# Expert rows taken by one-hot products inside the expert loop, and the attention bias on VectorE, in a hybrid block with 32 experts

## The chip, the cores and the metric

One core of a Trainium2 chip runs the whole block in one launch. The metric is the device time in microseconds, as the median of several runs. All tensors are fp32 in HBM. The core has TensorE (PE, with its weight loads as PEld), VectorE (DVE), ScalarE (ACT), GpSimd (POOL) and the queue of SyncE (SP), which issues nearly all loads.

## The reference

256 tokens of width 1024 pass one layer: a norm, three branches (a short convolution, attention with 8 heads of 64, a gated linear attention), a gated merge, an output projection, and a mixture of 32 experts of which each token takes two.

```python
h = rms_norm(x, norm_mix); parts = split(h @ w_in)              # w_in: 1024 x 4624
# attention, causal, T = 256, one block
s = q @ k.T * scale + table[:, t5_bucket(q_pos - k_pos)]        # -inf above the diagonal
y_attn = softmax(s) @ v
merged = sum(sigmoid(h @ w_merge_gate[n]) * (y_n @ w_branch[n]) for n in 3 branches)
x = x + merged @ w_out
h2 = rms_norm(x, norm_ffn)
group = argmax(h2 @ w_rg + b_rg)                                # 4 groups of 8 experts
top_p, top_i = top_k(softmax(le of that group), 2)
weights = p_group_top * top_p / sum(top_p)
for each expert e, with xs = the rows of h2 that chose e:
    ys = (silu(xs @ w_g[e]) * (xs @ w_u[e])) @ w_d[e]           # 1024 -> 512 -> 1024
x = x + sum over the two choices of weights * ys
```

## The kernel before

It is written engine by engine, with semaphores by hand, so the order on each engine is the order of the text. Line numbers are those of the profile.

**The dense part.** Twenty weight matrices of 2 MB (L424 to L428) pass through five slots of SBUF, `ring`. ScalarE rounds each quarter to fp32r (`high_pre`, L700) and VectorE takes the rest (`low_pre`, L1404), and TensorE makes three fp32r products in place of one in fp32 (L988 to L990 by feature, L966 to L968 by token). Ten half-matrix products, `dense[u]`, are interleaved with the eight heads (L1131 to L1138). After each stand the scores of head u (`scores`), the transposes of the probabilities of head u-1 (`turn_prob`) and the products with v of head u-2 (`prob_v`). A head's scores are a product of a reversing matrix `antid` with the bias rows (L1103) and one of q and k (L1104), summed in PSUM. q is kept zero outside its head's 64 rows, so that these products use all 128 rows. VectorE takes the row maximum from PSUM (`row_max`, L1546), ScalarE the exponential, VectorE scales by the row sum (`prob_scale`, L1552, L1555).

**Output projection and routing.** `out_proj` (L1169 to L1171) writes four banks. VectorE adds them to x, TensorE transposes the new x (`turn_x1`) and multiplies it with the router's weights (`route`, L1193), VectorE picks the experts (`pick`), and small products count the slot of every choice (L1219), which VectorE reads as `slotf` (L1720). Slots are sorted by expert. `seed` (L1186) puts x into the four banks in which the result is summed.

**The gather.** VectorE builds two one-hot matrices of 128 tokens by 512 slots, `perm` (L1724, L1725). Eight groups of four fp32r products (L1253 to L1265) make x of all 512 slots, which ScalarE and VectorE copy to `xs`. Then in the loop GpSimd copies the 64 columns of each expert out of `xs` into `xe` (L660).

**The expert loop.** One pass runs over 32 experts. Each has six units of weights of 1 MB: gate and up in two halves, down in two halves. They land in a ring of 20 units (`unit`), in the order of `order` (L451 to L456). SP issues a load when the unit 20 places before has been used (`unit_free`). The first 20 loads (`first_load`) wait for the regions of SBUF that the dense part still holds. On TensorE one turn of the loop is: first half of gate and up of expert e (L1293, L1295, which write the two halves of the columns and so run side by side), the transposes of expert e-1's product (`turn_h`, L1308), the sums of expert e-2 into the four banks (`combine`, L1346), second half of gate and up, and the down products of expert e-1 (L1332; L1328 for the last).

Of the kernel before, what the change touches and what calls it, by code (L numbers as in the profile page):

```python
# [56 lines left out]
GATHER = (0, 1, 2, 0, 1, 2, 1, 2)  # L57
# [4 lines left out]
SPAD = SLOTS + WIN  # L62
# [14 lines left out]
RING = 20  # L77
# [19 lines left out]
def hybrid_block(nc, x, rel_bias_table, norm_mix, w_in, conv_w, conv_b, q_norm, k_norm, w_gla_alpha,  # L97
# [17 lines left out]
    with ctx:  # L115
# [26 lines left out]
        antid = place("antid", [P, P], F32)  # L142
# [24 lines left out]
        stat = place("stat", [P, 64], F32)  # L167
        reset = place("reset", [P, T], F32)
# [3 lines left out]
        rsum = place("rsum", [P, NH, TT], F32)  # L172

# [12 lines left out]
        iota_g = place("iota_g", [P, NE], F32)  # L186
        jcol = place("jcol", [P, MAXWIN], F32)
        slotf = place("slotf", [P, TT, TOPK], F32)
        wts = place("wts", [P, TT, 2], F32)
        offf = place("offf", [1, MAXWIN * NE + 1], F32)  # L190
        off_tab = place("off_tab", [1, MAXWIN * NE + 1], I32)
# [10 lines left out]
        here_at = [region]  # L202
        sig0 = here("sig0", [P, KD, T], F32)
# [14 lines left out]
        small_at = region + 6 * 4 * UNIT + 4 * KD * SPAD  # L218
        out_hi = [w_hi, [place(f"out_hi{c}", [P, CW], F32R, at=small_at + 4 * CW * c) for c in range(CHUNKS)]]
# [9 lines left out]
        gv_at = here_at[0]  # L229
        gv = here("gv", [P, TT, C], F32)  # L230
# [20 lines left out]
        here_at = [region]  # L251
        spare_at = [region, region + 4 * UNIT]
        here_at[0] += 2 * 4 * UNIT
        xs_at = here_at[0]
        xs = here("xs", [P, KD, SPAD], F32)
        fin = place("fin", [P, TT, D], F32, at=xs_at)
        spare_at += [here_at[0] + 4 * UNIT * i for i in range(4)]
        here_at[0] += 4 * 4 * UNIT
        xe = []
        for b in range(2):  # L260
            perm_at = here_at[0]
            xe.append(here(f"xe{b}", [P, KD, WIN], F32))
        back_at = here_at[0]
        assert back_at == small_at + 4096
        g_act = here("g_act", [P, C], F32)
        y_hi = here("y_hi", [P, C], F32R)
        w_hit = here("w_hit", [P, TOPK, T], F32)
        back = [here(f"back{b}", [P, T], F32R) for b in range(2)]
        assert here_at[0] == back_at + 4 * TT * D
        xn_hi = place("xn_hi", [P, TT, D], F32R, at=back_at)  # L270
        junk = place("junk", [P, D], F32, at=spare_at[0] + 4 * D)
        xn_lo = place("xn_lo", [P, TT, D], F32R, at=spare_at[0])
        he = here("he", [P, KC, WIN], F32)
        slot_row = here("slot_row", [P, TOPK, T], F32)
        perm = [place(f"perm{b}", [P, SLOTS], F32R, at=at) for b, at in enumerate((here_at[0], perm_at))]
        w_row = here("w_row", [P, TOPK, T], F32)
# [4 lines left out]
        iota_s = place("iota_s", [P, SLOTS], F32, at=w_al_at)  # L281
        y_lo = place("y_lo", [P, C], F32R, at=w_al_at)

        unit_at = [ring_at[s] + 4 * UNIT * j for s in range(3) for j in range(2)] + [spare_at[1]] + spare_at[2:]
        unit_at += [ring_at[3], ring_at[3] + 4 * UNIT, w_hi_at, w_hi_at + 4 * UNIT]
        unit_at += [ring_at[4], ring_at[4] + 4 * UNIT, xn_at, x_at, spare_at[0]]
# [42 lines left out]
        xn_lo_ready = sem("xn_lo_ready")  # L329
# [3 lines left out]
        xs_act = sem("xs_act")  # L333
        xs_dve = sem("xs_dve")
# [54 lines left out]
        perm_ready = sem("perm_ready")  # L389
        route_ready = sem("route_ready")  # L390
        gather_mm = sem("gather_mm")
        iota_ready = sem("iota_ready")
# [6 lines left out]
        seeded = sem("seeded")  # L399
        slot_ready = sem("slot_ready")  # L400
# [13 lines left out]
        first_act = sem("first_act")  # L414
        first_dve = sem("first_dve")
# [36 lines left out]
        for e in range(1, NE):  # L452
            halves = [[(kind, e, c) for kind in ("g", "u")] for c in range(2)]
            downs = [("d", e - 1, c) for c in range(2)]
            order += halves[0] + (downs + halves[1] if e == NE - 1 else halves[1] + downs)
# [96 lines left out]
        def _(pool):  # L552
# [80 lines left out]
            for h in range(NH):  # L633
                if h >= 4:
                    pool.wait_ge(score_mm, h - 3)
# [1229 lines left out]
```

## Time and profile before

| | |
|---|---|
| median of 3 runs | 764.85 us (764.61 to 765.08) |
| profiled execution | 764.3 us, of which the span is 762.6 us |
| PE busy | 689.7 us, 90% of the span |
| DVE, ACT, POOL busy | 303.3, 199.7, 44.4 us |
| moved by DMA | 247.39 MB |
| first gate product of expert 0 | 312.93 us from the start |

The profile shows one execution. "Busy" is the time in which an engine had an instruction in flight, and matmul ends are modelled, so that the distance between the starts of two matmuls says more than the duration of one. Each fp32 matmul leaves two records. 128\*64 behind a matmul means that it uses 128 rows and 64 columns of the array, 64\*128 means 64 rows and all columns. The chain is followed back from the last instruction, and names at each step what released it.

### The profile page before, as it was taken

What the parts mean: (1) busy time and instruction counts of PE and PEld (TensorE: products, weight loads), DVE (VectorE), ACT (ScalarE), POOL (GpSimd) and SP (SyncE); (2) the same over time, 40 slices, a digit from 0 to 9 for tenths busy, and PEclk for the clock granted to TensorE, in tenths of its full rate; (3) what the DMA queues carried; (4) which work ended last, traced back from release to release, by engine and by line L of the source; (5) the groups of instructions that cost most, each with busy time, mean ns of one, the idle gap of its engine ahead of it and who ended that gap; (6) DMA issues with size and microseconds to landing.
All of it is one profiled execution on the core that took longest, in us unless ns stands there. A gap on an engine that the chain in (4) does not pass through costs nothing.

```text
span 762.6 us, 10123 instructions
## 1 busy us (share of the span) xinstructions
PE 689.7 (90%) x3888; PEld 410.0 (54%) x3888; DVE 303.3 (40%) x512; ACT 199.7 (26%) x308; POOL 44.4 (6%) x89
## 2 busy tenths in 40 slices
PE   4999999999999999999999998798879888987895
PEld 3977799899999877533333333233323323332332
DVE  5357777754545666422322222311221212122212
ACT  4275355363434533211111111111011111111011
POOL 7002100000000000000000000000000000000000
PEclk9999999999999999999999999999999999999998
DMA  8963463454555389699999999999999999999993
GB/s 245 371 228 124 158 195 125 127 169 149 152 186 217 138 362 390 236 423 421 421 420 421 422 419 423 420 422 422 419 419 423 420 422 422 421 422 421 421 419 141
DMA packets 50175, 247.39 MB, mean 324 GB/s; under 512 B 5592, under 2 KB 5680, under 8 KB 25680
## 3 DMA queue, kind: packets, MB, share of 16 engines
q1 hardware_dynamic: 48672, 245.45, 81.2%
q0 software_dynamic: 912, 1.25, 0.9%
q8 instruction: 31, 0.51, 0.3%
q10 hardware_dynamic: 544, 0.06, 0.1%
q14 instruction: 16, 0.13, 0.0%
HBM read 245.67 MB, written 1.06 MB: 324 GB/s over the span
## 4 chain that ended last, share of the span: by engine, by line
PE 59%; DMA 29%; DVE 5%; SPq 3%; ACT 2%; issue 1%; DVEq 0%; ACTq 0%
DMA unit<-in_w_expert_up 28%; PE ps L1293 16%; PE ps L1332 7%; PE ps L988 6%; PE ps L990 6%; PE ps L989 6%; SPq L499 3%; PE ps L1346 2%; PE ps L966 2%; PE ps L968 2%; PE ps L967 2%; DVE ring_lo L1404 1%; ACT w_hi L700 1%; PE ps L1169 1%; PE ps L1171 1%
## 5 line engine op out<-in xcount | busy, mean ns | idle before, releaser
L1293 PE MATMUL ps<-unit,xe 128*64 128x512 f32 x512 | 245.2, 625 | 44.7 <-DMA unit<-in_w_expert_up 44.7
L1295 PE MATMUL ps<-unit,xe 128*64 128x512 f32 x512 | 246.0, 626 | 0.0
L1293 PEld LDWEIGHTS ps<-unit,xe 128*64 128x64 f32 x512 | 68.8, 142 | 194.4 <-issue 194.2
L1791 DVE TENSOR_TENSOR g_act<-g_act,ps 64x512 f32<-64x512 f32 x32 | 34.6, 1081 | 243.2 <-ACT g_act L889 240.0
L1404 DVE TENSOR_TENSOR ring_lo<-ring,w_hi 128x1024 fp32r<-128x1024 f32 x76 | 91.4, 1223 | 53.9 <-ACT w_hi L700 52.6
L1332 PE MATMUL ps<-unit,he 128*64 128x512 f32 x496 | 111.9, 592 | 0.0
L988 PE MATMUL ps<-hT_hi,w_hi 128*128 128x256 f32 x320 | 92.0, 287 | 2.7 <-DVE ring_lo L1404 2.7
L700 ACT ACTIVATE w_hi<-ring 128x1024 fp32r<-128x1024 f32 x76 | 79.0, 1057 | 47.3 <-PE ps L990 34.9
L989 PE MATMUL ps<-hT_lo,w_hi 128*128 128x256 f32 x320 | 90.5, 283 | 0.0
L990 PE MATMUL ps<-hT_hi,ring_lo 128*128 128x256 f32 x320 | 90.4, 283 | 0.0
L1332 PEld LDWEIGHTS ps<-unit,he 128*64 128x64 f32 x496 | 37.0, 137 | 69.2 <-issue 64.6
L1295 PEld LDWEIGHTS ps<-unit,xe 128*64 128x64 f32 x512 | 68.8, 142 | 0.0
L988 PEld LDWEIGHTS ps<-hT_hi,w_hi 128*128 128x128 f32 x320 | 61.3, 192 | 5.3 <-issue 5.1
L990 PEld LDWEIGHTS ps<-hT_hi,ring_lo 128*128 128x128 f32 x320 | 61.2, 191 | 0.0
L989 PEld LDWEIGHTS ps<-hT_lo,w_hi 128*128 128x128 f32 x320 | 61.2, 191 | 0.0
L1816 DVE SCALAR_TENSOR_TENSOR y_lo<-ps,w_slot,y_hi 128x512 fp32r<-128x512 f32 (+1 forms) x32 | 23.8, 742 | 88.1 <-ACT y_hi L907 88.1
L898 ACT ACTIVATE he<-ps 128x256 f32<-128x256 f32 x32 | 12.3, 385 | 154.8 <-PE ps L1308 154.8
L889 ACT ACTIVATE g_act<-ps 64x512 f32<-64x512 f32 x32 | 18.9, 589 | 129.5 <-PE ps L1295 129.5
L907 ACT ACTIVATE y_hi<-ps,w_slot 128x512 fp32r<-128x512 f32 (+1 forms) x32 | 21.8, 681 | 96.9 <-PE ps L1332 93.0
L660 POOL COPY xe<-xs 128x512 f32 x31 | 19.1, 616 | 398.7 <-PE ps L1295 380.7
L1346 PE MATMUL ps<-y_hi,back 64*128 64x512 f32 x128 | 34.6, 437 | 1.7 <-DVE y_lo L1821 1.7
L966 PE MATMUL ps<-w_hi,hT_hi 128*128 128x512 f32 x80 | 32.3, 404 | 1.3 <-DVE ring_lo L1404 1.2
(295 smaller groups left out, 799.2 us busy)
## 6 DMA issues: line engine op xcount, KB each, us to landing
unit<-in_w_expert_gate SPq DMA_DIRECT2D x64, 1024.0 KB, 26.9
unit<-in_w_expert_up SPq DMA_DIRECT2D x64, 1024.0 KB, 26.6
unit<-in_w_expert_down SPq DMA_DIRECT2D x63, 1024.0 KB, 26.6
ring<-in_w_in SPq DMA_DIRECT2D x9, 2048.0 KB, 14.2
ring<-in_w_merge_gate SPq DMA_DIRECT2D x6, 2048.0 KB, 10.7
ring<-in_w_branch SPq DMA_DIRECT2D x3, 2048.0 KB, 8.8
ring<-in_w_out SPq DMA_DIRECT2D x2, 2048.0 KB, 8.5
x_tok<-in_x SPq DMA_DIRECT2D x2, 512.0 KB, 4.4
```

The lines of the kernel that those rows point to most:

```text
L700: s_.activation(w_hi[c][:, :], ring[g % PRE_RING][:, chunk(c)], ACT.Copy).then_inc(wpre_hi, 1)
L966: t_.matmul(bank(b), x_hi[:, k, rows], wh, start=(k == 0), stop=False)
L988: t_.matmul(o, wh, x_hi[:, k, :], start=(k == 0 and j == 0), stop=False, skip_group_check=True)
L989: t_.matmul(o, wh, x_lo[:, k, :], start=False, stop=False, skip_group_check=True)
L990: ins = t_.matmul(o, wl, x_hi[:, k, :], start=False, stop=(k == nk - 1), skip_group_check=True)
L1293: gate = t_.matmul(ps[0:WIN, b, :], xe[b][:, k, :], ug[:, C * j:C * (j + 1)], start=(k == 0), stop=(k == KD - 1))
L1295: up = t_.matmul(ps[WIN:P, b, :], xe[b][:, k, :], uu[:, C * j:C * (j + 1)], start=(k == 0), stop=(k == KD - 1))
L1332: ins = t_.matmul(ps[half * WIN:(half + 1) * WIN, 3, :], he[:, k, :], u[:, D * j + C * half:D * j + C * (half + 1)], start=(k == 0), stop= ...
L1346: ins = t_.matmul(bank(4 + 2 * tt + half), back[e % 2][rows, tt * P:(tt + 1) * P], part[rows, :], start=False, stop=True, skip_group_check ...
L1404: v.tensor_tensor(ring_lo[g % PRE_RING][:, chunk(c)], ring[g % PRE_RING][:, chunk(c)], out_hi[g == 19][c][:, :].bitcast(F32), ALU.subtract ...
L1791: v.tensor_tensor(g_act[0:WIN, :].rearrange("p (k f) -> p k f", k=KC), g_act[WIN:P, :].rearrange("p (f k) -> p k f", k=KC), ps[WIN:P, e % ...
L1816: v.scalar_tensor_tensor(out=y_lo[:, 0:cols], in0=bank(3)[:, 0:cols], scalar=w_slot[:, e % 2:e % 2 + 1], in1=y_hi[:, 0:cols].bitcast(F32), ...
```

## The change

In the dense part:

- A pair of heads is computed together. Scores use 64 rows for each of the two heads, with no product for the bias. `row_max` is one VectorE instruction that adds the bias, writes the sum to SBUF and takes the maximum, and one that negates it. `scores` and `prob_v` run on every other turn. The order of queries is reversed in q and back in the result.
- In the linear attention the loops over the two row halves become inner loops.

At the output projection:

- The last of the four banks is computed as two of 256 columns, each added, squared and transposed by itself.
- The low part of the normed x is no longer made. x is scaled into `xn2` in fp32, in an order of columns in which each half of an expert's rows is contiguous.

At the experts:

- `perm`, `xs`, the eight gather groups and GpSimd's copies go. For each expert VectorE builds a one-hot matrix of 256 tokens by 64 places (`choose`), TensorE makes the 64 rows by four fp32 products (`pick_rows`), ScalarE copies them to SBUF (`rows_copy`), TensorE transposes them (`turn_rows`), and VectorE scales them into `xe` (`rows_in`). In the loop this is done for expert e+1 while expert e runs.
- The ring has 21 units at other addresses, and the first loads wait for other points.
- The last expert's order on TensorE and its order of loads are changed.

```diff
+            def pick_rows(i, e):
+                pe.wait_ge(chosen_ready, i + (e + 1))
+                for tt in range(TT):
+                    for c in range(2):
+                        ins = t_.matmul(ps[c * WIN:(c + 1) * WIN, e % 2, :], pick_w[e % 2][:, tt, :], xn2[:, tt, C * c:C * (c + 1)],
+                                        start=(tt == 0), stop=(tt == TT - 1))
+                ins.then_inc(picked, 1)
+            def turn_rows(i, e):
+                pe.wait_ge(rows_out, i + (e + 1))
+                pe.sem_inc(turning, 1)
+                for j in range(4):
+                    ins = t_.transpose(bank(e % 2, 4)[:, j, :], xr[:, j * P:(j + 1) * P], ident[:, :])
+                ins.then_inc(rows_turned, 1)
...
             with pe.Fori(0, passes) as p:
-                gate_up(p, 0, (0, 1))
+                gate_up(p, 0, (0,))
+                pick_rows(NE * p, 1)
+                gate_up(p, 0, (1,))
+                turn_rows(NE * p, 1)
...
                 for e in range(1, NE - 1):
                     gate_up(p, e, (0,))
                     turn_h(p, e - 1)
+                    pick_rows(NE * p, e + 1)
                     if e >= 2:
                         combine(p, e - 2)
                     gate_up(p, e, (1,))
+                    turn_rows(NE * p, e + 1)
                     down(p, e - 1)
                 gate_up(p, NE - 1, (0,))
                 turn_h(p, NE - 2)
                 combine(p, NE - 3)
-                down(p, NE - 2)
                 gate_up(p, NE - 1, (1,))
+                down(p, NE - 2, (0,))
+                turn_h(p, NE - 1)
+                down(p, NE - 2, (1,))
+                down(p, NE - 1, (0,))
                 combine(p, NE - 2)
-                turn_h(p, NE - 1)
-                down(p, NE - 1)
+                down(p, NE - 1, (1,))
                 combine(p, NE - 1)
...
+            def choose(i, e):
+                dve.wait_ge(picked, i + (e + 1))
+                v.scalar_tensor_tensor(out=both, in0=places, scalar=tab[:, 0, e:e + 1], in1=flat_slots, op0=ALU.add,
+                                       op1=ALU.is_equal).then_inc(same_ready, 1)
+                dve.wait_ge(same_ready, i + (e + 1))
+                v.tensor_tensor(pick_w[e % 2][:, :, :], same[:, :, 0, :], same[:, :, 1, :], ALU.add).then_inc(chosen_ready, 1)
+            def rows_in(i, e):
+                dve.wait_ge(rows_turned, i + (e + 2))
+                v.tensor_tensor(xe[e % 2][:, :, :, :], ps[:, e % 2, :].rearrange("p (j c n) -> p j c n", j=4, c=2),
+                                g_ffn[:, :].rearrange("p (c j) -> p j c", c=2).unsqueeze(3).broadcast_to([P, 4, 2, WIN]),
+                                ALU.mult).then_inc(xe_ready, 1)
...
                 for tt in range(TT):
-                    t_.matmul(o, antid[:, :], bias_h[:, h % 4, P * (1 - tt):T], start=True, stop=False)
-                    ins = t_.matmul(o, qTz[:, h, tt * P:(tt + 1) * P], kT[:, h // 2, keys], start=False, stop=True)
+                    for h in heads:
+                        rows = slice(DH * (h % 2), DH * (h % 2) + DH)
+                        ins = t_.matmul(ps[:, 4 + h % 2, P * tt:P + 2 * P * tt], qTz[rows, h, tt * P:(tt + 1) * P],
+                                        kT[rows, pair, 0:P * (tt + 1)], start=True, stop=True)
...
-                    ins = v.tensor_reduce(nmx[:, h, tt:tt + 1], ps[:, 4 + h % 2, P * tt:P + 2 * P * tt], AX_X, ALU.max,
-                                          negate=True)
+                    ins = v.tensor_tensor_reduce(prob[:, h % 2, P * tt:P + 2 * P * tt], ps[:, 4 + h % 2, P * tt:P + 2 * P * tt],
+                                                 bias_h[:, h % 4, P * (1 - tt):T], 1.0, -3e38, ALU.add, ALU.max,
+                                                 rmx[:, h, tt:tt + 1])
...
-                if n < 6:
-                    sp.wait_ge(proj_done, first_bank[NPRE - PRE_RING + n // 2 + 1])
+                if n < 5:
+                    sp.wait_ge(branch_done, 8)
                 elif n < 11:
+                    sp.wait_ge(proj_done, first_bank[NPRE - PRE_RING + (n - 5) // 2 + 1])
+                elif n == 11:
                     sp.wait_ge(branch_done, 12)
-                elif n < 15:
+                elif n < 16:
                     sp.wait_ge(proj_done, first_bank[NPRE - 2] + 3)
-                elif n < 18:
+                elif n < 20:
                     sp.wait_ge(proj_done, first_bank[NPRE])
-                elif n == 18:
+                else:
                     sp.wait_ge(seeded, 1)
                     sp.wait_ge(xn_hi_ready, TT)
-                    sp.wait_ge(xn_lo_ready, TT)
-                else:
-                    sp.wait_ge(gather_mm, KD)
```

**TensorE, one turn of the expert loop, before** (expert 2: from its last gate and up products of the first half to its first of the second; `g_act` is expert 1's product, `y_hi` and `y_lo` expert 0's output).

```order
L1293 MATMUL ps<-unit_177,xe_146 64x512
L1295 MATMUL ps<-unit_178,xe_146 64x512
L1302 REGISTER_ALU
L1308 MATMUL ps<-ident,g_act 128x64 x4
L1346 MATMUL ps<-y_hi,back_151 128x512 x2
L1346 MATMUL ps<-y_lo,back_151 128x512 x2
L1346 MATMUL ps<-y_hi,back_151 128x512 x2
L1346 MATMUL ps<-y_lo,back_151 128x512 x2
```

The same place in the changed kernel (its line 1219 is `pick_rows`, 1278 `turn_h`, 1318 `combine`).

```order
L1263 MATMUL ps<-unit_176,xe_149 64x512
L1265 MATMUL ps<-unit_177,xe_149 64x512
L1272 REGISTER_ALU
L1278 MATMUL ps<-ident,g_act 128x64 x4
L1219 MATMUL ps<-xn_143,pick_w_157 64x512 x4
L1318 MATMUL ps<-y_hi,back_154 128x512 x2
L1318 MATMUL ps<-y_lo,back_154 128x512 x2
L1318 MATMUL ps<-y_hi,back_154 128x512 x2
L1318 MATMUL ps<-y_lo,back_154 128x512 x2
```

Four products that write 64 rows of PSUM now stand between two groups that write 128. At the end of the same turn, where the down products followed on the second half at once, there are now four transposes (line 1228 is `turn_rows`, 1304 `down`).

```order
L1263 MATMUL ps<-unit_178,xe_149 64x512
L1265 MATMUL ps<-unit_179,xe_149 64x512
L1228 MATMUL ps<-ident,xr 128x128 x4
L1304 MATMUL ps<-unit_180,he 64x512 x4
L1304 MATMUL ps<-unit_181,he 64x512 x4
```

These write all 128 rows again between two groups that write 64.

**VectorE, the third head, before** (`nmx` are the negated row maxima, `ycT` the convolution that follows).

```order
L1571 TENSOR_TENSOR conv_u<-ycT,ps 128x2x256
L1546 TENSOR_REDUCE nmx<-ps 128x1 x2
L1578 TENSOR_SCALAR ycT<-conv_u,cw_sb,cb_sb 128x256
L1581 SCALAR_TENSOR_TENSOR ycT<-conv_u,cw_sb,ycT 128x256 x2
L1578 TENSOR_SCALAR ycT<-conv_u,cw_sb,cb_sb 128x256
```

And in the changed kernel (`aqk` holds the probabilities, `gqk` the bias, ISA is the custom instruction with its read of the accumulator).

```order
L1565 TENSOR_TENSOR conv_u<-ycT,ps 128x2x256
L1536 ISA aqk,rmx<-ps,gqk 128x128
L1536 ISA rmx 128x1
L1536 ISA aqk,rmx<-ps,gqk 128x256
L1536 ISA rmx 128x1
L1540 TENSOR_SCALAR nmx<-rmx 128x2
L1572 TENSOR_SCALAR ycT<-conv_u,cw_sb,cb_sb 128x256
```

Two instructions have become five between the same neighbours, and the custom ones also write the sum of scores and bias to SBUF.

## Rows read from the trace of the kernel before

**Rows 1.** The page's 40 slices of the span: DMA share in tenths.
```profile
DMA  8963463454555389699999999999999999999993
```

**Rows 2.** Busy time by stretch: us, PE, PEld, DVE, ACT, POOL (instructions), PEclk, DMA share, GB/s.
```profile
325.00:445.00 120.00, 120.00 (x610) 44.20 (x608) 33.52 (x60) 16.62 (x30) 6.17 (x10) 1.00 1.01 421
445.00:745.00 300.00, 255.31 (x1206) 96.46 (x1204) 67.51 (x121) 33.92 (x61) 11.72 (x19) 0.95 1.01 421
```

**Rows 3.** Waits: who waited for whom, us in total, times, longest.
```profile
PE ps L1293 <- DMA unit<-in_w_expert_up: 44.7, 21, 3.6
```

**Rows 4.** The chain, 335 to 360 us: start, us, what.
```profile
339.25 3.43 PE ps L1332 x16
...
351.07 3.43 PE ps L1332 x16
```

**Rows 5.** PE in order of time, expert 1: start, us, line, out<-in, array part, shape.
```profile
322.85 0.59 PE L1293 MATMUL ps<-unit,xe 128*64 128x512 f32 x1
...
323.38 0.46 PE L1308 MATMUL ps<-ident,g_act 64*128 64x64 f32 x4
...
324.25 0.59 PE L1293 MATMUL ps<-unit,xe 128*64 128x512 f32 x1
```

**Rows 6.** PE in order of time, last expert's second half and expert 30's sums.
```profile
747.91 0.59 PE L1293 MATMUL ps<-unit,xe 128*64 128x512 f32 x1
...
749.27 0.39 PE L1346 MATMUL ps<-y_lo,back 64*128 64x512 f32 x2
```

**Rows 7.** PE in order of time, fourth turn of the attention.
```profile
132.11 0.38 PE L1103 MATMUL ps<-gqk,antid 128*128 128x128 f32 x2
...
133.42 0.49 PE L1112 MATMUL ps<-ident,aqk 128*128 128x128 f32 x3
133.84 0.65 PE L1124 MATMUL ps<-aqk,av 128*64 128x256 f32 x2
...
134.86 0.28 PE L989 MATMUL ps<-hT_lo,w_hi 128*128 128x256 f32 x1
```

**Rows 8.** PE in order of time, fifth turn of the attention, with its idle time.
```profile
141.70 0.49 PE L1112 MATMUL ps<-ident,aqk 128*128 128x128 f32 x3
...
143.41 0.62 PE L1124 MATMUL ps<-aqk,av 128*64 128x256 f32 x2 [1.22 <-DVE ya_lo L1563]
```

**Rows 9.** DVE in order of time, the head before that turn.
```profile
135.14 0.61 DVE L1546 TENSOR_REDUCE nmx<-ps 128x1 f32<-128x128 f32 x2
...
138.84 0.29 DVE L1555 TENSOR_SCALAR aqk<-aqk,rsum 128x128 f32<-128x128 f32 x1
```

**Rows 10.** One line: duration min/median/max ns, first and last start.
```profile
L1663 DVE CUSTOM_DVE_ANT_0 junk<-x_tok x3: 691/691/1226, 279.4 to 293.7; 128x512 f32<-128x512 f32 x2, 128x1024 f32<-128x1024 f32 x1
```

**Rows 11.** DVE, ACT and PE in order of time, slots to first expert.
```profile
299.50 0.28 DVE L1720 TENSOR_REDUCE slotf<-hits 128x4 f32<-128x128 f32 x1
...
301.04 0.60 ACT L873 ACTIVATE slot_row<-ps 128x512 f32<-128x512 f32 x1 [1.55 <-PE ps L1237]
...
311.95 1.05 PE L1237 MATMUL ps<-ident,wts 128*128 128x128 f32 x8
312.93 0.64 PE L1293 MATMUL ps<-unit,xe 128*64 128x512 f32 x1
```

**Rows 12.** DVE in order of time, a 512-wide product out of PSUM.
```profile
124.03 0.69 DVE L1571 TENSOR_TENSOR conv_u<-ycT,ps 128x512 f32<-128x512 f32 x1 [2.72 <-PE ps L990]
```

**Rows 13.** The chain's end: start, us, what.
```profile
750.39 0.44 PE ps L1308 x4
751.29 3.70 PE ps L1328 x32
```

**Rows 14.** DMA issues on SP in order of time.
```profile
285.12 0.33 SPq L499 DMA_DIRECT2D unit<-in_w_expert_up  x1
```

**Rows 15.** PE in order of time, where transposes and sums meet.
```profile
357.98 0.50 PE L1346 MATMUL ps<-y_hi,back 64*128 64x512 f32 x1
358.04 0.29 PE L1308 MATMUL ps<-ident,g_act 64*128 64x64 f32 x2
```

More of the change, by code:

```diff
@@ L229, in hybrid_block @@
         gv_at = here_at[0]
+        out_hi = [w_hi, [place(f"out_hi{c}", [P, CW], F32R, at=gv_at + 4 * CW * c) for c in range(CHUNKS)]]
         gv = here("gv", [P, TT, C], F32)
@@ L454, in hybrid_block @@
             downs = [("d", e - 1, c) for c in range(2)]
[L455 removed]
+            order += halves[0] + halves[1] + downs
         order += [("d", NE - 1, c) for c in range(2)]
@@ L914, in _ @@
             with act.Fori(0, passes) as p:
+                with act.If(p > 0):
+                    rows_copy(NE * p, 0)
+                rows_copy(NE * p, 1)
+                act.wait_ge(route_ready, 1)
+                act.reg_load(passes, npass[0:1, 0:1])
+                turns = act.value_load(npass[0:1, 0:1], min_val=1, max_val=MAXWIN)
                 silu(p, 0)
@@ L1167, in out_proj, with turn_x1 @@
                         pe.wait_ge(wpre_lo, CHUNKS * (18 + half) + k // CHUNK_T + 1)
[L1168 to L1171 removed]
+                    wh, wl = weights(18 + half, k * C + (n if part == 1 else 0), n)
+                    t_.matmul(o, merged_hi[:, k, rows], wh, start=(k == 0), stop=False)
+                    t_.matmul(o, merged_hi[:, k, rows], wl, start=False, stop=False)
+                    ins = t_.matmul(o, merged_lo[:, k, rows], wh, start=False, stop=(k == KD - 1))
                 if ks[-1] == KD - 1:
[L1173 to L1181 removed]
+                    ins.then_inc(part_done if part == 0 else proj_done, 1)
+            def turn_x1(tt, ks, added):
+                pe.wait_ge(x1_ready, added)
+                for k in ks:
+                    ins = t_.transpose(bank(4 + 2 * tt + k // 4, 4)[:, k % 4, :], x_tok[:, tt, k * P:(k + 1) * P], ident[:, :])
                 ins.then_inc(x1_turned, 1)
@@ L1273, in _ @@
             pe.sem_inc(combined, 8)
+            pe.sem_inc(picked, 2)
+            pe.sem_inc(rows_turned, 1)
+            seed(1, 0)
+            rows(slotf, slot_ready, 2)
+            pe.wait_ge(xn_hi_ready, TT)
+            pick_rows(0, 0)
+            seed(1, 1).then_inc(seeded, 1)
+            turn_rows(0, 0)
+            pe.wait_ge(table_ready, 1)
+            rows(wts, wts_ready, 3)
             passes = pe.alloc_register("passes_pe")
```

452 lines of the change are left out of this document (197 added, 255 removed).

## The prediction

> **What bounds the kernel now.** I read the slices first, then busy time by stretch, then the waits, the chain, and last the order of time at the seams. From 325 us to the end of the weights the DMA share is full and 421 GB/s flow [rows 1, 2]. TensorE is busy for all of 325 to 445 us and for 255.3 of the next 300 us, and its waits for units sum to 44.7 us [rows 2, 3]. So it first works off the ring's lead at its own pace, which the chain shows as 351.07 - 339.25 = 11.82 us for one expert [rows 4]. Then the transfers set the pace: six units of 1.0486 MB at 421 GB/s are 6 x 2.49 = 14.94 us for one expert. Before 312.9 us the dense part, the routing and the gather run, nearly all on TensorE. What the change does is therefore three sums: how much earlier the loop starts, what one turn costs TensorE, and whether that turn is still shorter than its transfers once the lead is counted.
>
> **The start of the loop: the attention.** A head's scores take 133.42 - 132.11 = 1.31 us, its transposes 0.33, its products with v 0.43 + 0.22 of work, and from the last transpose (133.75) to the steady pace of the dense products (134.86 less one step of 0.12) there are 0.99 us [rows 7]. So going from the full array to 64 columns and back costs 0.99 - 0.65 = 0.34 us. A pair of heads costs 2 x (1.31 + 0.99) = 4.60 us now. Afterwards its scores are half of one head's, 0.65, with the same 0.34 for the change of shape, and its products with v 0.99 if the two heads run side by side: 1.98. Four pairs save 10.5 us, and the idle 1.22 us of the fifth turn, in which TensorE waits for VectorE [rows 8], goes. Against that VectorE gets more to do while the turns get shorter. Its row maximum takes 0.61 us [rows 9]; the custom form costs 0.69 us for 512 columns and 1.23 for 1024 [rows 10], so about 0.15 + 0.13 per 128: for 128 and 256 columns, two reads of the accumulator and the negation I take 1.0 us. At the fourth head the probabilities are ready at 139.4 and taken at 141.70 [rows 8, 9], a slack of 2.3 us. TensorE gains 1.3 us per turn on it from the third on, and the in-order VectorE loses 0.4 per head. I let TensorE wait 1.1 us there and 1.6 at the sixth head, after which it recovers. The linear attention's rearranged halves give 0.4. Together 10.5 + 1.2 - 2.7 + 0.4 = 9.4 us; with no wait 12, with twice the waits 7.
>
> **The start of the loop: the gather.** Slots are ready at 299.78, the loop starts at 312.93 [rows 11]. Now the split last bank hides half of its addition, square and transpose, but 0.9 us of routing products move ahead of its end: I take nothing for it (-0.7 to +0.7). After the slots: the row products of eight records (0.9, as the 312.93 - 311.95 = 0.98 of the later ones less a change of shape) to 300.85, `pick_rows` 1.71 (below) to 302.6, the copy on ScalarE 0.60 [rows 11] with 0.2 on either side to 303.5, four transposes 0.44 and a signal to 304.1, the product into `xe` 0.7 [rows 12] to 304.9, start at 305.1. That saves 7.8 us. The new start is 312.93 - 9.4 - 7.8 = 295.7.
>
> **One turn on TensorE.** The pace of a gate and up pair is 0.43 us for each of its records, and sixteen records of the down products take 3.43 [rows 4, 5], so one fp32 product of 512 columns that shares the array with a neighbour costs 0.43, 24 such steps are 10.3, and 11.82 - 10.3 = 1.54 is left for `turn_h` and `combine`. What is added:
> - `pick_rows`: two token halves times two column halves, the latter side by side as gate and up are. Four steps of 0.43 = 1.71 us. If they didn't run side by side, 3.42.
> - It parts `turn_h` from `combine`. Alone, `turn_h` costs from 323.28 (322.85 + 0.43) to 323.82 (324.25 - 0.43) = 0.54 us [rows 5], for four transposes of 0.055 each: 0.32 is the change to 64 rows and back. Alone, `combine` takes from 748.34 to 749.27 + 0.24 = 1.17 us and about 0.15 for the way back [rows 6]. Together 1.86 instead of 1.54: +0.3.
> - `turn_rows`: four transposes of 0.11 = 0.44, and the way to the full array and back again, 0.34 [rows 7]: +0.78.
>
> The turn becomes 11.82 + 1.71 + 0.3 + 0.78 = 14.6 us. A gain is excluded, since work is only added; if the shape changes cost nothing it is 11.82 + 1.71 + 0.44 = 13.97, if each seam costs another 0.04 it is 14.8. The rows measure these very seams, so I take 14.6 (14.45 to 14.75). ScalarE and VectorE get 1.3 and 1.4 us more per turn and have the room: what `pick_rows` waits for, `choose`, stands behind the low part of the last output, which I see done 1.9 us into a turn, and ends at 2.7, while `pick_rows` comes at 4.0.
>
> This row-based seam has a rule beside it: the Trainium skill, "TensorEngine Tiling (Array Packing)", Key Properties, says that a change of the tiling mode, as against a change of tile, drains the engine. By that rule each turn goes from two such changes to six, and the sum is the 14.6 above; by the skill's Theoretical Speedup alone, with no drain, it would be 13.97. The trace agrees with the drain: 0.32 us around 0.22 of transposes.
>
> **The sum.** First two experts, to the first product of expert 2: five half gate and up or down groups at 3.43 (17.15), two `pick_rows` (3.42), `turn_h` 0.54, `turn_rows` 0.63 and 0.78, and 0.95 of exposed copy into `xe`, which nothing covers the first time: 23.5 us, to 319.2. Then 29 turns: 423.4, to 742.6. The last expert: 3.43, 1.54, 3.43; then the product behind silu, 750.39 - 748.34 = 2.05 [rows 6, 13], transposes 0.45 (half of expert 30's down products lie beside that wait), two half down groups 3.43, the sums of expert 30 1.4, and from the start of the last half down group to the end 762.6 - 751.29 - 1.72 = 9.6 [rows 13]: 25.3 us. The span is 767.9, against 762.6: +5.3 us. The profiled execution took 764.3, so 769.6; from the median of 764.85 it is 770.
>
> Does the DMA come in? Unit 12 was issued at 285.12 [rows 14]; that wait comes 9.4 earlier, and flows from about 277.7. The other 180 units at 2.49 end at 726. TensorE reaches its last gate and up units at about 747. So the transfers are over some 40 us before the end, and the earlier loads and the 21st unit buy nothing: of 14.94 us per expert the turn now takes 14.6, and the lead that it used to work off in eleven experts is never worked off.
>
> **Rivals.**
> - *The transfers stay the bound* (what the earlier loads, 726 instead of 748, would give). After the last half unit there are 0.9 us of products and 7.7 of tail: 734.5, in the median 737. It needs a turn below 13.1 us, which is less than the work alone. Chance 0.03.
> - *The seams are hidden*: a turn nearer 13.97 us, 29 x 0.63 = 18 us less: 752. For it speaks that the first sums start before the last transpose of `turn_h` is through [rows 15], so that work on unlike shapes can overlap; against it the lone `turn_h`. It decides from 14.3 us: below that the kernel is faster. Chance 0.16.
> - *The dense part gives all it can* (12 us rather than 9.4) and the turn is 14.5: 770 - 2.6 - 2.9 = 764.5, the same. Chance 0.11 for this and its neighbours.
> - *The picks run one after the other*, or each turn waits for VectorE: +1.71 x 31 = 53 us, 823. The code of the pairs is that of gate and up. Chance 0.04.
>
> **How the numbers follow.** The forecast, a turn of 14.45 to 14.75 with 7 to 12 us from the attention, has 0.66 and spans 763 to 777. About 0.2%, 1.5 us, is what a measurement of this kernel can tell. Slower by more: 0.66 + 0.04 = 0.70. Same: 0.11. Faster: 0.19. The range takes part of the second rival in: 757 to 778.
>
> **What would show it.** The spacing of the first down record of two experts in mid-loop: 14.6 us. The first gate product at 295.7, of which 9.4 at the end of the heads. No wait of TensorE for units, a granted clock of full rate throughout the loop, where now it falls to half after waits (mean 0.95 [rows 2]). DMA slices that are empty over the last 35 to 40 us. The forecast is wrong if turns come at less than 14.3 us, or if TensorE still waits for weights.

## The result, and the profile after

The changed kernel takes 767.86 us (median of 4 runs, 767.72 to 767.99) against 764.73 us for the kernel before on the same chip (763.25 to 765.08): 0.45% slower, ratio 1.0045, 95% interval 1.003 to 1.006. The forecast was 770 us, slower with 0.70, range 757 to 778. The profiled execution has a span of 766.0 us, against 762.6.

Start with the page of the kernel after: busy time, then three rows of the slices (PE busy, TensorE's clock, DMA share), each digit a fortieth of the span.

```profile
PE 737.8 (96%) x4232; PEld 410.2 (54%) x4232; DVE 339.5 (44%) x617; ACT 218.4 (29%) x335; POOL 23.9 (3%) x53
...
PE   3999999999999899999999999999999999999996
...
PEclk9999999999999999999999999999999999999999
DMA  9954446435579469999999999999999999999901
```

The end of the DMA row is what answers [rows 1]: there it stayed at 9 up to the last slice but one, here two slices are nearly empty. The stretches answer [rows 2] (us, PE, PEld, DVE, ACT, POOL busy, PEclk, DMA share, GB/s; the second stretch ends just before the last `down` of the loop's 30 turns), and three more show where the transfers end.

```profile
325.00:445.00 120.00, 120.00 (x596) 42.56 (x590) 37.85 (x72) 18.39 (x33) 0.00 (x0) 1.00 1.01 419
445.00:736.00 291.00, 291.00 (x1438) 103.10 (x1436) 94.61 (x180) 44.90 (x80) 0.00 (x0) 1.00 0.99 409
...
700.00:728.00 28.00, 28.00 (x140) 10.13 (x142) 8.37 (x16) 4.52 (x8) 0.00 (x0) 1.00 0.98 408
...
729.00:740.00 11.00, 11.00 (x58) 4.16 (x58) 2.47 (x4) 1.57 (x3) 0.00 (x0) 1.00 0.04 14
740.00:766.00 26.00, 18.82 (x114) 7.94 (x110) 7.88 (x15) 4.55 (x9) 0.00 (x0) 0.96 0.10 41
```

TensorE is busy for every microsecond of these two stretches, at full clock; before, it was so for 85% of the second stretch at 0.95. Its 44.7 us of waits for units [rows 3] are gone: the list of waits holds no wait of TensorE for a unit. The DMA share is 0.98 up to 728 us and falls away over the next three, so the transfers are over some 35 to 38 us before the end. The bound has changed sides: from the weight stream to TensorE.

The seams of one turn, TensorE in order of time (start, us, line; the gate and up rows lie in the gaps). L1304 is `down`, L1278 `turn_h`, L1219 `pick_rows`, L1318 `combine`, L1263 gate, L1228 `turn_rows`:

```profile
444.55 0.66 PE L1228 MATMUL ps<-ident,xr 128*128 128x128 f32 x4
445.13 3.65 PE L1304 MATMUL ps<-unit,he 128*64 128x512 f32 x16
...
452.15 0.46 PE L1278 MATMUL ps<-ident,g_act 64*128 64x64 f32 x4
452.54 1.94 PE L1219 MATMUL ps<-xn,pick_w 128*64 128x512 f32 x8
454.41 0.50 PE L1318 MATMUL ps<-y_hi,back 64*128 64x512 f32 x2
...
455.53 0.64 PE L1263 MATMUL ps<-unit,xe 128*64 128x512 f32 x1
...
459.11 0.66 PE L1228 MATMUL ps<-ident,xr 128*128 128x128 f32 x4
459.70 3.65 PE L1304 MATMUL ps<-unit,he 128*64 128x512 f32 x16
```

From `down` to `down` are 459.70 - 445.13 = 14.57 us, where [rows 4] showed 11.82. `pick_rows` takes 454.41 - 452.54 = 1.87, `turn_rows` with its way there and back 0.59 + 0.10. That makes 2.56 of the 2.75 us added; the other 0.19 lie in the parted `turn_h` and `combine` and in the first steps behind a change of shape. The same 14.57 lies between the chain's entries at 314.04 and 736.68: (736.68 - 314.04) / 29 = 14.574.

The start of the loop, in order of time from the slots on, answers [rows 11]:

```profile
284.10 4.19 ACT L799 ACTIVATE xn<-x_tok,stat 128x1024 f32<-128x1024 f32 x2 [0.29 <-DVE stat L1668]
...
287.40 0.29 DVE L1714 TENSOR_REDUCE slotf<-hits 128x4 f32<-128x128 f32 x1
...
288.21 1.05 PE L1210 MATMUL ps<-ident,slotf 128*128 128x128 f32 x8
...
289.20 1.94 PE L1219 MATMUL ps<-xn,pick_w 128*64 128x512 f32 x8
...
293.94 0.61 PE L1263 MATMUL ps<-unit,xe 128*64 128x512 f32 x1 [0.41 <-DVE xe L1735]
```

Slots are ready at 287.69 instead of 299.78, the loop starts at 293.94 instead of 312.93: 19.0 us earlier. And yet the kernel isn't faster. From the loop's first product to the end it takes 766.0 - 293.9 = 472.1 us, where before it took 762.6 - 312.9 = 449.7: 22.4 more. TensorE's turn of 14.57 us is now nearly as long as the 14.94 of the transfers, but it holds from the first expert on, while before the ring's lead let the first experts go at 11.82.

### The profile page after: what moved, and what is told of

The parts are those of the page before. It is cut to its first block, busy times and chain, and to the rows that moved or that the text cites. A ratio compares the mean times of both kernels' runs of the same rounds, so it can differ in the third digit from the quotient of the medians.

```text
span 766.0 us, 10774 instructions
## 1 busy us (share of the span) xinstructions
PE 737.8 (96%) x4232; PEld 410.2 (54%) x4232; DVE 339.5 (44%) x617; ACT 218.4 (29%) x335; POOL 23.9 (3%) x53
## 3 DMA queue, kind: packets, MB, share of 16 engines
HBM read 245.67 MB, written 1.06 MB: 322 GB/s over the span
## 4 chain that ended last, share of the span: by engine, by line
PE 86%; DVE 6%; ACT 4%; DMA 2%; issue 1%; DVEq 0%; SPq 0%; ACTq 0%
PE ps L1263 29%; PE ps L1304 14%; PE ps L1219 8%; PE ps L950 5%; PE ps L952 5%; PE ps L951 5%; PE ps L1318 5%; DVE ring_lo L1387 3%; PE ps L1228 2%; PE ps L928 2%; PE ps L930 2%; PE ps L929 2%; PE ps L1278 2%; DMA ring<-in_w_in 2%; ACT w_hi L654 1%
## 5 line engine op out<-in xcount | busy, mean ns | idle before, releaser
L1263 PE MATMUL ps<-unit,xe 128*64 128x512 f32 x512 | 231.8, 595 | 1.2 <-DVE xe L1735 1.2
L1265 PE MATMUL ps<-unit,xe 128*64 128x512 f32 x512 | 231.8, 595 | 0.0
L1263 PEld LDWEIGHTS ps<-unit,xe 128*64 128x64 f32 x512 | 67.5, 137 | 140.0 <-issue 139.0
L1735 DVE TENSOR_TENSOR xe<-ps,g_ffn 128x512 f32<-128x512 f32 x32 | 22.1, 692 | 216.6 <-PE ps L1228 216.6
L1304 PE MATMUL ps<-unit,he 128*64 128x512 f32 x496 | 113.4, 598 | 0.0
L1265 PEld LDWEIGHTS ps<-unit,xe 128*64 128x64 f32 x512 | 67.5, 137 | 0.0
L1304 PEld LDWEIGHTS ps<-unit,he 128*64 128x64 f32 x496 | 32.8, 136 | 58.2 <-issue 58.2
L1219 PE MATMUL ps<-xn,pick_w 128*64 128x512 f32 x256 | 62.0, 604 | 0.0
```

What stands on the lines that cost most here:

```text
L1219: ins = t_.matmul(ps[c * WIN:(c + 1) * WIN, e % 2, :], pick_w[e % 2][:, tt, :], xn2[:, tt, C * c:C * (c + 1)], start=(tt == 0), stop=(tt = ...
L1263: gate = t_.matmul(ps[0:WIN, b, :], xe[b][:, j, c, :], ug[:, C * j:C * (j + 1)], start=(k == 0), stop=(k == KD - 1))
L1265: up = t_.matmul(ps[WIN:P, b, :], xe[b][:, j, c, :], uu[:, C * j:C * (j + 1)], start=(k == 0), stop=(k == KD - 1))
L1304: ins = t_.matmul(ps[half * WIN:(half + 1) * WIN, 3, :], he[:, k, :], u[:, D * j + C * half:D * j + C * (half + 1)], start=(k == 0), stop= ...
```

## The experiments

Times are medians. The kernel before ran beside each group of experiments on the same chip (763.8, 764.2 and 764.1 us, 764.0 for experiment 8), and the ratios are to these times. Differences from the changed kernel are against its 767.9.

**1. The attention alone, in the kernel before.** Only the hunks of the attention and the linear attention are taken over, in short:

```diff
-            for par in range(2):
-                for tt in range(TT):
-                    for a in range(2):
+            for tt in range(TT):
+                for a in range(2):
+                    for par in range(2):
...
-                    t_.matmul(o, antid[:, :], bias_h[:, h % 4, P * (1 - tt):T], start=True, stop=False)
...
-                    ins = v.tensor_reduce(nmx[:, h, tt:tt + 1], ps[:, 4 + h % 2, ...], AX_X, ALU.max, negate=True)
+                    ins = v.tensor_tensor_reduce(prob[:, h % 2, ...], ps[:, 4 + h % 2, ...], bias_h[:, h % 4, ...],
+                                                 1.0, -3e38, ALU.add, ALU.max, rmx[:, h, tt:tt + 1])
```

> The kernel before with the attention of the change alone (heads in pairs, bias added on VectorE, the halves of the linear attention in the new order); gather, loop and 20 units are those of before. The changed kernel passed the end of the heads 12 us earlier than before. My theory: in the kernel before, the weight transfers bound the loop, and each starts when TensorE frees a buffer, so the whole stream moves earlier with the dense part: the loop's first product at 301 (before 312.9), the time 753 us, 12 less. Rival: the stream of 192 units is what counts and its start is set by the ring, so earlier products only lengthen TensorE's waits: 764 to 765, no change. By my prediction's own term (9.4 us) it would be 755.5.

Measured: 753.8 us, ratio 0.9865 (0.985 to 0.988). Its first gate product, TensorE in order of time, stands 10.9 us earlier than in the kernel before:

```profile
302.01 0.64 PE L1295 MATMUL ps<-unit,xe 128*64 128x512 f32 x1
```

And its waits for units (us in total, times, longest) sum to about what they were [rows 3]:

```profile
PE ps L1295 <- DMA unit<-in_w_expert_up: 46.4, 22, 3.0
```

So the attention is a gain by itself, and the stream of a transfer-bound kernel moves with it: first theory right, the rival wrong. All the rest of the change, of which the rows taken in the loop are the main part, costs 767.9 - 753.8 = 14 us. The rest also has the split last bank, the loads, the 21st unit and the last expert's order; only the unit is taken apart below.

**2. The attention undone, in the changed kernel** (the same hunks, reversed; no diff of its own).

> The changed kernel with the attention of before (one head at a time, bias through TensorE). If the attention part is worth the same to a kernel that TensorE bounds as its 10 us in the kernel that the transfers bound, or its full 12 us earlier start: 768 + 10 to 12 = 778 to 780, first gate product at 306. Rival (part of the earlier start is lost again on the way, in the gather): 772 to 776.

Measured: 780.6 us, ratio to before 1.021 (1.019 to 1.023), first gate product at 305.89. The attention is worth 12.8 us here and 10.1 there: the two halves of the change add up to within 3 us (what the 3 us are, no run shows), and nothing of the earlier start was lost in the gather, since the first product moved by 305.89 - 293.94 = 12.0. With the attention of before, the rest costs 780.6 - 764.1 = 16.5 us.

**3. Picks before the transposes of h.**

```diff
                     gate_up(p, e, (0,))
-                    turn_h(p, e - 1)
+                    pe.wait_ge(h_ready, NE * p + (e + 2))
                     pick_rows(NE * p, e + 1)
+                    turn_h(p, e - 1)
```

> The changed kernel with one edit: in each of the 30 turns the products that pick the rows stand directly behind the first half of gate and up, and the transposes of h behind them, next to combine. All products are the same; the array is cut to another shape two times less in each turn. My theory (TensorE's turn of 14.57 us is the bound and each parting of turn_h from combine costs 0.3 us): turn 14.27, time 767.9 - 29 x 0.3 = 759. Rival (changes of shape are hidden, the turn is made of work alone): 14.57, 768.

Measured: 759.6 us, ratio to before 0.994 (0.993 to 0.995). The turn (`turn_rows` to `turn_rows`) is 14.28 us. TensorE in order of time shows why:

```profile
464.64 1.89 PE L1219 MATMUL ps<-xn,pick_w 128*64 128x512 f32 x8
466.46 0.33 PE L1278 MATMUL ps<-ident,g_act 64*128 64x64 f32 x2
466.57 0.50 PE L1318 MATMUL ps<-y_hi,back 64*128 64x512 f32 x1
466.63 0.29 PE L1278 MATMUL ps<-ident,g_act 64*128 64x64 f32 x2
```

The last transposes and the first sums stand between each other again, as in [rows 15]; the picks, which use the array in the shape of gate and up, start on their beat (0.43 after the last pair). Nothing was removed but two changes of shape: 0.29 us a turn, 8.3 us in all. This one order makes the changed kernel 0.6% faster than the one before.

**4. Half of the picks.** The rows of the last 128 tokens stay out of the experts' input.

```diff
-                for tt in range(TT):
+                for tt in range(TT - 1):
```

> The changed kernel with the products that pick the rows taken over the first 128 tokens only (rows of the other tokens stay out of the experts' input), so half of each pick_rows goes. My theory (TensorE's own work is the turn, pairs side by side): the turn is 0.86 us shorter, 13.71, and the time 768 - 31 x 0.86 = 741, with the transfers near their end then. Rival (the turn is set by waits for VectorE or ScalarE, or picks don't run side by side): 0 or 1.7 us per turn, that is 768 or 716 at most, the latter stopped by the transfers at about 737.

Measured: 743.4 us. The turn is 13.72, 0.85 less, from rows of `turn_h` at 443.80, 457.51 and 471.23. Work on TensorE is what the turn is made of. The sum 767.9 - 31 x 0.85 = 741.5 is missed by 2, of which 1.3 are waits for units that come back.

**5. Rows turned by halves, behind `combine`.** Experiment 3's order, and:

```diff
-                for j in range(4):
-                    ins = t_.transpose(bank(e % 2, 4)[:, j, :], xr[:, j * P:(j + 1) * P], ident[:, :])
+                for c in range(2):
+                    rows = slice(WIN * c, WIN * c + WIN)
+                    for j in range(4):
+                        at = 256 * (1 - c) + WIN * j
+                        ins = t_.transpose(ps[:, 2 if c == 0 else e % 2, at:at + WIN], xr[rows, j * P:(j + 1) * P], ident[rows, rows])
...
                         combine(p, e - 2)
+                    turn_rows(NE * p, e + 1)
                     gate_up(p, e, (1,))
-                    turn_rows(NE * p, e + 1)
                     down(p, e - 1)
```

The two halves go to different PSUM banks, `rows_in` reads them in two products, ScalarE copies the rows before `he`, and TensorE waits for `he` before it writes to its bank; experts 0 and 1 are turned as before.

> The previous order (picks before the transposes of h), and the picked rows are turned in eight transposes of 64 rows, directly behind combine, instead of four of 128 rows between gate/up and down; the lower half of the rows is turned into another bank. So the array is changed to 64 rows once in a turn and back once, instead of three times each as in the changed kernel. My theory: against the changed kernel -0.3 (as the kernel with that order alone) and -0.34 (the way to the full array and back), turn 13.93, time 768 - 29 x 0.64 = 749. Rival (seams are free): 768. Third: the transposes now stand 1.6 us behind the picks and wait for ScalarE's copy of the rows, which gives back up to 0.5 us a turn: 755 to 764.

Measured: 747.5 us, ratio to before 0.978 (0.977 to 0.980). TensorE in order of time:

```profile
449.52 0.52 PE L1330 MATMUL ps<-y_lo,back 64*128 64x512 f32 x2
449.88 0.46 PE L1238 MATMUL ps<-ident,xr 64*128 64x64 f32 x8
450.27 0.64 PE L1275 MATMUL ps<-unit,xe 128*64 128x512 f32 x1
...
463.72 0.47 PE L1238 MATMUL ps<-ident,xr 64*128 64x64 f32 x8
464.12 0.64 PE L1275 MATMUL ps<-unit,xe 128*64 128x512 f32 x1
```

The turn is 13.85: 0.43 less than in experiment 3, where 0.34 for the way to the full array and back had been forecast. Eight transposes of 64 rows cost 450.27 - 449.88 = 0.39 us against 0.69 for four of 128 with their two seams: 0.30 of the 0.43. Where the other 0.13 went the rows above don't say. The list of waits has none for the copy of the rows, and a single one of 0.7 us for `he`.

**6. The same, halves in turn.** `for j` outside, `for c` inside, so that neighbours lie on different row halves.

> The previous best (picks before the transposes of h, rows turned in 64-row transposes behind combine, 13.85 us a turn, 747.5 us) with these transposes in alternating order, upper and lower half of the rows in turn, instead of four and four. If neighbours on different row halves run side by side, 0.2 of their 0.39 us go: turn 13.65, 742. Rival (transposes don't overlap, or the turn there waits for ScalarE's copy): 747.5. The transfers are over at 729 us in the previous kernel, TensorE's last products at 742: they bind nothing at 742 yet.

Measured: 746.3 us, ratio 0.977 (0.975 to 0.978), the fastest version of this study with the whole computation. The gain forecast for it isn't there: the turn is 13.78, 0.07 less, and from the start of the last sums to the next gate product it is 448.71 - 448.02 = 0.69 against 450.27 - 449.52 = 0.75.

```profile
448.02 0.52 PE L1330 MATMUL ps<-y_lo,back 64*128 64x512 f32 x2
448.25 0.53 PE L1238 MATMUL ps<-ident,xr 64*128 64x64 f32 x8
448.71 0.64 PE L1275 MATMUL ps<-unit,xe 128*64 128x512 f32 x1
```

The gain of 1.2 us is small (runs of 745.3 to 747.2 against 747.3 to 748.1), and the loop doesn't account for it. The 29 x 0.07 = 2 us that the turns save are lost again in the last two, where 1.4 us of waits for units come back: from the first gate product to the end both traces have 451.3 us (745.2 - 293.9 and 746.1 - 294.8). The 0.9 us between the two starts lies in the part that is the same in both; over the experiments that keep the changed kernel's dense part this start varies from 293.3 to 295.0. So eight transposes in turn save 0.06 us against eight in a row, not 0.2; why is open.

**7. The picks in the other order.** My fourth rival had the picks run one after the other, so I ordered them so:

```diff
-                for tt in range(TT):
-                    for c in range(2):
+                for c in range(2):
+                    for tt in range(TT):
```

> The changed kernel with the same eight records of picks in another order: both token halves of one column half, then both of the other, so that neighbours in the program no longer go to different halves of the array. The rival of my prediction in which the picks run one after the other, made on purpose. If two products side by side are what makes a pick_rows cost 1.82 us, it now costs 2.7 (the middle two may still overlap) to 3.4 us, 0.9 to 1.6 more, and the time is 768 + 31 x 0.9 to 1.6 = 796 to 818. Rival (TensorE reorders or the order of a program doesn't matter): 768.

Measured: 768.2 us, the turn 14.58. My theory was wrong. The weight loads in order of time show four loads at once and then two and two, as in the changed kernel:

```profile
452.76 0.20 PEld L1219 LDWEIGHTS ps<-xn,pick_w 128*64 128x64 f32 x4
453.25 0.15 PEld L1219 LDWEIGHTS ps<-xn,pick_w 128*64 128x64 f32 x2 [0.28 <-issue]
453.68 0.15 PEld L1219 LDWEIGHTS ps<-xn,pick_w 128*64 128x64 f32 x2 [0.28 <-issue]
```

Two products of the lower half stand ahead, four records, and still eight records take four steps of 0.43 us. These rows don't name the halves, but records of one half can't account for it: experiment 8 has them 0.43 us apart. So the upper half's first record starts beside the lower half's. The Trainium skill, "TensorE: Matmul & The Clock Gate", The mechanism (Part 3), has it that products start strictly in program order and only weight loads are pulled ahead; between two column halves of the array this trace doesn't agree, and experiment 8 shows it by line. How far ahead was open, so:

**8. Gates, then ups.**

```diff
                     for j in range(4):
                         k = 4 * c + j
                         gate = t_.matmul(ps[0:WIN, b, :], xe[b][:, j, c, :], ug[:, C * j:C * (j + 1)], ...)
+                    for j in range(4):
+                        k = 4 * c + j
                         up = t_.matmul(ps[WIN:P, b, :], xe[b][:, j, c, :], uu[:, C * j:C * (j + 1)], ...)
```

> The changed kernel with the four gate products of a unit pair first and then the four up products, instead of gate and up in turn. With the four picks, the order of the program didn't matter. If products for the other half of the array are started past two products that wait, but not past four (eight instructions with their weight loads), half of the overlap goes: a half group of 3.43 us becomes 4.3 to 5.2 us, two in each turn, and the time is 768 + 60 x 0.9 to 1.7 = 820 to 870. Rival (each half of the array takes its own products from a queue that reaches further): 3.43 us, 768.

Measured: 879.3 us, ratio 1.151 (1.149 to 1.153). The products of one half group, and below them its weight loads, each in order of time (L1263 gate, L1267 up):

```profile
467.05 2.31 PE L1263 MATMUL ps<-unit,xe 128*64 128x512 f32 x5
468.77 0.64 PE L1267 MATMUL ps<-unit,xe 128*64 128x512 f32 x1
469.20 0.59 PE L1263 MATMUL ps<-unit,xe 128*64 128x512 f32 x1
...
470.11 2.31 PE L1267 MATMUL ps<-unit,xe 128*64 128x512 f32 x5
```

```profile
467.05 0.14 PEld L1263 LDWEIGHTS ps<-unit,xe 128*64 128x64 f32 x1 [0.29 <-issue]
...
468.77 0.14 PEld L1263 LDWEIGHTS ps<-unit,xe 128*64 128x64 f32 x1 [0.29 <-issue]
468.77 0.19 PEld L1267 LDWEIGHTS ps<-unit,xe 128*64 128x64 f32 x2
...
470.11 0.14 PEld L1267 LDWEIGHTS ps<-unit,xe 128*64 128x64 f32 x1 [0.29 <-issue]
```

Four gate records go alone, four go beside the first four ups, and four ups go alone: twelve steps of 0.43 = 5.16 us instead of 3.43, and 64 such groups x 1.72 = 110 us, to 878. The upper end of my range for each group was right; the time lies above my 870 because I had counted 60 groups. Together the two runs give the reach: a product of the other half is started past four records that stand ahead of it, and not past eight; in experiment 8 it started when four were left, beside the first of them.

**9. Rows taken already turned.** x as the weight, the choice as what moves; `turn_rows` and the copy fall away:

```diff
+                for k in range(KD):
+                    at = WIN * (2 * (k % 4) + k // 4)
+                    for tt in range(TT):
+                        ins = t_.matmul(ps[:, e % 2, at:at + WIN], xn2[:, tt, P * k:P * (k + 1)], pick_w[e % 2][:, tt, :],
+                                        start=(tt == 0), stop=(tt == TT - 1))
```

> The changed kernel with the one-hot products the other way round: x is the weight (128 tokens by 128 columns) and the choice of 64 rows is what moves, so that the rows come out already turned. Sixteen products of 64 columns behind the second half of gate and up take the place of pick_rows, of ScalarE's copy and of turn_rows. The array is changed to full size once in a turn; combine stands next to turn_h again. If a product costs its columns (a full-size fp32 transpose of 128 columns takes 0.11 us, so 0.055 to 0.11), the turn is 11.82 + 0.34 + 16 x 0.055 to 0.11 = 13.0 to 13.9 and the time 737 to 749. Rival (the load of 128 x 128 fp32 weights for every product sets the pace, 0.19 us as the weight loads of the dense part show): 11.82 + 0.34 + 3.04 = 15.2, 786.

Measured: 802.9 us, ratio 1.051 (1.050 to 1.052). Both theories too low. TensorE in order of time:

```profile
453.54 3.79 PE L1215 MATMUL ps<-pick_w,xn 128*128 128x64 f32 x32
457.25 3.65 PE L1299 MATMUL ps<-unit,he 128*64 128x512 f32 x16
...
469.22 3.79 PE L1215 MATMUL ps<-pick_w,xn 128*128 128x64 f32 x32
```

The turn is 15.68. Sixteen products are 32 records of 3.71 / 32 = 0.116 us, the step of an fp32r record of 256 columns in the dense part (0.118). A record of the full array has its own weight load of 0.19 us, and at 64 columns it costs no less than at 256. I had counted one step for a product where the trace has two records.

**10. Twenty units.** The ring without its 21st.

```diff
-RING = 21
+RING = 20
```

> The changed kernel with a ring of 20 units instead of 21. My theory (the transfers are 35 us ahead at the end and bind nothing): no change, 768 +- 1, and the issue-to-landing time of a unit stays near 15 us. Rival (the ring's lead still matters, as in the kernel before): a unit's 2.5 us later at the end, 770 or more.

Measured: 767.8 us, no change. The 21st unit buys nothing while TensorE is the bound. The earlier first loads are still in this kernel; that they buy nothing either follows only from there being no wait for a unit.

**11. Less work than the transfers.** Experiment 6 with the picks of experiment 4.

> The kernel with rows turned side by side (13.78 us a turn, 746.3 us) with its picks over the first 128 tokens only, as in the kernel with half the picks (the other tokens' rows stay out of the experts' input). TensorE alone would need 746 - 31 x 0.86 = 719 or so. My theory: now the transfers bind again, at the 734.5 + 2.5 = 737 that my prediction gave its first rival, and TensorE waits for units again. Rival (the transfers have more room than I think): 720 to 730.

Measured: 743.8 us, the time of experiment 4 (743.4), although its first turns take 12.92 us against 13.72. TensorE's waits for units are back:

```profile
PE ps L1275 <- DMA unit<-in_w_expert_up: 19.2, 10, 2.4
```

The last of them, TensorE in order of time:

```profile
701.02 0.61 PE L1275 MATMUL ps<-unit,xe 128*64 128x512 f32 x1 [2.25 <-DMA unit<-in_w_expert_up]
```

The mechanism is that of my first rival, its number was 7 us too low. The last wait is for a unit of expert 30, and from there to the end are 741.8 - 701.0 = 41 us in which TensorE waits for no unit: the last units arrive faster than the last two experts' products, sums and waits use them. The DMA share falls away between 726 and 732 us in experiments 4 to 6 and here, as in the changed kernel. Two kernels with 0.8 us between their turns end within 0.5 us of each other, so I take 743 to 744 us as the floor of this order of work, and experiment 6 is within 3 us of it.

## Why the prediction was right

Step by step, the forecast beside what the profile of the changed kernel shows:

- *Loop start, 295.7:* 293.94. The attention was put at 9.4; the part up to the slots, with the split last bank, gave 299.78 - 287.69 = 12.1, which was the bound I gave for "no wait". The attention alone moved the loop's start by 10.9 (experiment 1) and 12.0 us (experiment 2), more than 9.4 both ways. The step that failed is the term for VectorE's lateness, 2.7 us of waits at the fourth and sixth head: TensorE waited 0.9 us for it in all. The linear attention's halves gave 1.4, not 0.4: TensorE's products that follow it start at 64.43 instead of 65.82 (64.83 in experiment 1, so 1.0 to 1.4). The row that shows the longer of the two waits:

```profile
150.66 0.55 PE L1075 MATMUL ps<-ident,aqk 128*128 128x128 f32 x3 [0.69 <-DVE aqk L1547]
```

- *Slots to loop, 5.3 us:* 6.25, so the gather gave 6.9 and not 7.8. A seed product that I had not counted stands ahead of the row products (they begin at 288.21, 0.5 after the slots), and the first `pick_rows` took 1.87 with its seams, not 1.71.
- *One turn, 14.6 us:* 14.57. Its terms: `pick_rows` 1.71 as work (half of it is worth 0.85, experiment 4), the parting of `turn_h` from `combine` 0.3 (0.29, experiment 3), `turn_rows` 0.78 (0.43 of it can be saved by another shape and place, experiment 5). That changes of shape cost time is thereby shown, and the rival of hidden seams is out. What I had brought forward for that rival was misread: the transposes and the sums in [rows 15] both stand as 64\*128, so their overlap says nothing of work on unlike shapes. The rule of the Trainium skill that the prediction weighed ("TensorEngine Tiling (Array Packing)", Key Properties: a change of mode drains the engine) agrees with these 0.29 us.
- *First two experts 23.5:* from 293.94 to the first gate product of expert 2 at 317.45, 23.51. *29 turns 423.4:* from there to 740.10, 422.65. *Last expert 25.3:* 25.9. The sum of 767.9 for the span was 1.9 too high, by the start.
- *Transfers over at 726, some 40 us before the end:* 728 to 731, 35 to 38 us.
- *The rivals:* transfers stay the bound: no wait for a unit, though the 737 that I gave for it should have been 744 (experiment 11). The pair of "12 us from the dense part" and "a turn of 14.5" came half: the 12 us did, the turn didn't, and the time lies between that case's 764.5 and the forecast. Picks one by one: no, and at four products order alone can't bring it about (experiment 7).

In short: 29 x (14.57 - 11.82) = 80 us of new work on TensorE. Where it went shows in the 29 turns between the transposes of expert 1's product and those of expert 30's. In the kernel before, TensorE in order of time has them here:

```profile
334.23 0.33 PE L1308 MATMUL ps<-ident,g_act 64*128 64x64 f32 x2
...
738.56 0.33 PE L1308 MATMUL ps<-ident,g_act 64*128 64x64 f32 x2
```

That is 404.3 us, 61.6 more than 29 x 11.82. Of these, 44.7 are the waits [rows 3]. The other 17 are, by my estimate, time lost at the lower clock behind the waits, as in these rows of the kernel before:

```profile
465.04 1.09 PE L1293 MATMUL ps<-unit,xe 128*64 128x512 f32 x1 [2.87 <-DMA unit<-in_w_expert_up]
...
465.92 1.06 PE L1293 MATMUL ps<-unit,xe 128*64 128x512 f32 x1
...
466.78 1.06 PE L1293 MATMUL ps<-unit,xe 128*64 128x512 f32 x1
```

Behind the wait of 2.87 us the steps are 0.86 us instead of 0.43. In the changed kernel neither the waits nor the slow steps are left, so 62 of the 80 us cost nothing and the 29 turns take 422.7 us, 18.3 more. The first two experts add 5.8, and the new order of the last one gives 1.7 back. The loop became 22.4 us longer, the start gave 19.0 back, and 3.4 us are the loss in span.

## What to carry to other kernels

Work moved onto an engine that waits is free only up to the pace of the other side: sum what the engine does in one turn, changes of the array's shape included, and hold it against the transfers of a turn and the lead they start with. Then order the pieces by shape: moving and splitting the same work was worth 20 us here, more than the whole change lost. And price the halves of a change apart, since here one was a gain of 10 us and the other a loss of 14.

## What the runs showed of the hardware

- Products on two column halves of the array run side by side though four records of one half stand ahead of the other's first in the program; with eight ahead, the first four run alone (turn 14.58 against 14.57 in experiment 7; 5.16 against 3.43 us for a group in experiment 8).
- With 128 x 128 weights, a record of an fp32 product of 64 columns takes 0.116 us (experiment 9) and one of an fp32r product of 256 columns 0.118.
- Parting two groups of 64-row work by work of another shape costs 0.29 us; the way to the full array for four transposes and back takes 0.69 us in all, where eight 64-row transposes next to other 64-row work take 0.39 (experiments 3 and 5).
- Behind a wait of 2.87 us of TensorE the steps of gate and up were 0.86 us instead of 0.43, and the granted clock of 465 to 470 us was 0.66 in the mean, between the full rate and half of it; in the changed kernel, whose loop has no such wait, it was 1.00.
- A read of 128 x 1024 with a step of eight elements took ScalarE 2.14 us (4.19 for two), where one in order took 1.06 (the rounding of a weight quarter). It wasn't on the path here.
